# A convolution's later half moved into the gather stage, with the tiles of the recurrence reordered

## The reference, cut to what matters

```python
proj = h @ w_in[l]                       # hq, hf, hi, hg, cb, cc, ch, gates
...
o = hgrn2_chunkwise(rs(q), rs(k), rs(log_f), rs(hi))     # gated linear recurrence, chunks of 64
y_a = o_normed * silu(hg)
y_b = cb * causal_depthwise_conv(cc * ch, conv_w[l])     # 3 taps over positions, 512 channels
g_a, g_b = jnp.split(jax.nn.sigmoid(gates), 2, axis=-1)
merged = g_a * (y_a @ w_branch_hg[l]) + g_b * (y_b @ w_branch_conv[l])
x = x + merged @ w_out[l]
x = x + peer_ffn(rmsnorm_2(x, norm_ffn_g[l]), ...)

def peer_ffn(h, w_query, keys1, keys2, expert_u, expert_v):   # 8 heads, 2 x 128 keys, top 16
    q = (hf @ w_query).reshape(t, 8, 2, 128)
    s1, s2 = q[:, :, 0] . keys1, q[:, :, 1] . keys2
    v1, i1 = top_k(s1, 16); v2, i2 = top_k(s2, 16)            # then the best 16 of the 256 sums
    act = gelu(sum(expert_u[idx] * h))                        # 16384 experts, one row each of u and v
    out = sum(gate * act * expert_v[idx])
```

## Time and profile before

| what | us |
|---|---|
| median of 3 runs | 3173.85 (3169.38 to 3179.24) |
| profiled execution, its own time | 3174.83 |
| profiled execution, span of the trace | 3173.0 |
| start of level 1 of the mixer, from the span's start | 1516.35 |
| first gather issued, from the span's start | 1802.73 |

### The profile page before, as it was taken

One profiled execution on the slowest core, in us unless ns is written; L12 is line 12 of the kernel. 1 busy time (PEld: TensorE's weight loads), 2 busy tenths in 40 slices (PEclk: granted clock), 3 DMA queues, 4 the chain that ended last, 5 costly groups with the idle time before them and its releaser, 6 DMA issues. The chain is left out here.

```text
span 3173.0 us, 27344 instructions
## 1 busy us (share of the span) xinstructions
PE 2729.6 (86%) x9860; PEld 1403.3 (44%) x9860; DVE 1350.5 (43%) x3242; ACT 584.0 (18%) x1350; POOL 718.6 (23%) x622
## 2 busy tenths in 40 slices
PE   8999697787778878669999889999999877778887
PEld 6755333333333333244558756655555433333332
DVE  2162300000000000055422466676766777777774
ACT  2132100000000000012101123222322322222222
POOL 0000010000000000001440133443434444444442
PEclk9899799999999899879999999999999999999889
DMA  4003699999999999531114599999999999999997
GB/s 144 27 20 124 261 427 426 427 426 426 426 425 422 421 415 421 214 129 42 60 47 146 193 426 426 426 426 424 408 426 424 406 427 427 427 427 427 427 427 302
DMA packets 136982, 1043.17 MB, mean 329 GB/s; under 512 B 21824, under 2 KB 22672, under 8 KB 46352
## 3 DMA queue, kind: packets, MB, share of 16 engines
q0 software_dynamic: 82944, 545.32, 41.1%
q1 hardware_dynamic: 53904, 496.11, 38.2%
HBM read 1045.54 MB, written 20.97 MB: 336 GB/s over the span
## 5 line engine op out<-in xcount | busy, mean ns | idle before, releaser
L2132 PE MATMUL psum<-peer_ring,peer_diag 128*128 128x512 f32 x1824 | 861.2, 626 | 139.9 <-ACT peer_diag L2186 139.8
L2001 POOL DMA_INDIRECT peer_ring<-in_peer_uv,peer_pick x456 | 508.0, 1114 | 846.7 <-PE psum L2132 650.3
L2292 DVE CUSTOM_DVE_ANT_0 peer_ring<-peer_ring,sb_rows 128x1024 f32<-128x1024 f32 x456 | 556.9, 1225 | 327.7 <-DMA peer_ring<-in_peer_uv,peer_pick 319.8
L2132 PEld LDWEIGHTS psum<-peer_ring,peer_diag 128*128 128x128 f32 x1824 | 358.5, 200 | 603.1 <-issue 400.4
L1118 PE MATMUL psum<-ffn1w_w,sb_y 128*64 128x512 f32 x1872 | 509.6, 654 | 93.6 <-DMA ffn1w_w<-in_w_up 52.1
L1163 DVE TENSOR_TENSOR sb_y<-psum,sb_y 128x512 f32<-128x512 f32 x32 | 22.1, 692 | 877.0 <-ACT sb_y L1146 877.0
L1118 PEld LDWEIGHTS psum<-ffn1w_w,sb_y 128*64 128x64 f32 x1872 | 176.6, 149 | 361.0 <-issue 359.3
L2186 ACT ACTIVATE peer_diag<-sb_ident,peer_mix 128x128 f32<-128x128 f32 x512 | 177.4, 393 | 665.2 <-DVE peer_mix L2302 662.1
L1139 PE MATMUL psum<-ffn1w_w,moe_hT 128*64 128x512 f32 x864 | 227.9, 598 | 35.9 <-DVE moe_hT L1168 35.9
L1497 PE MATMUL psum<-sb_y,sb_tiles 128*128 128x512 f32 (+1 forms) x640 | 227.5, 514 | 19.2 <-PEq L104 18.5
L1211 POOL DMA_INDIRECT expert_rows<-sb_tiles,ffn_block_tok x32 | 32.2, 1007 | 894.8 <-ACT sb_tiles L1152 894.8
(11 more groups left out here) (427 smaller groups left out, 2697.6 us busy)
## 6 DMA issues: line engine op xcount, KB each, us to landing
ffn1w_w<-in_w_gate SPq DMA_DIRECT2D x64, 2048.0 KB, 33.1
ffn1w_w<-in_w_down SPq DMA_DIRECT2D x54, 2048.0 KB, 35.8
ffn1w_w<-in_w_up SPq DMA_DIRECT2D x53, 2048.0 KB, 33.9
sb_rows<-in_w_up SPq DMA_DIRECT2D x11, 2048.0 KB, 36.6
sb_tiles<-in_w_in2b SPq DMA_DIRECT2D x44, 512.0 KB, 3.4
sb_rows<-in_w_down SPq DMA_DIRECT2D x10, 2048.0 KB, 32.4
sb_tiles<-in_w_query SPq DMA_DIRECT2D x32, 512.0 KB, 7.7
sb_tiles<-in_w_out SPq DMA_DIRECT2D x24, 512.0 KB, 3.4
```

The costliest lines, as they stand in the source:

```text
L2001: pool.indirect_dma_start(out=row(n, 0, 2 * D), out_offset=None, in_=A["peer_uv"], in_offset=bass.IndirectOffsetOnAxis(ap=pick[:, i, j:j + ...
L2132: last = nc.tensor.matmul(ps[:, BANK[i] + c], diag[:, b % DIAGS, x], row(n, D + 512 * c, D + 512 * (c + 1)), start=False, stop=end, skip_g ...
L2292: dve.tensor_tensor_reduce(row(n, 0, D), row(n, 0, D), hr[:, i], 1.0, 0.0, ALU.mult, ALU.add, dots[:, i, j + x:j + x + 1]).then_inc(dotted, 1)
```

## The change

1. The convolution of the second half of the positions leaves the mixer. The 12 convolution tiles are multiplied at half width there; POOL works on 256 positions and keeps the last two columns of `cc * ch` in `halo`. In the gather stage the same 12 weight tiles are loaded again and multiplied with the second half's activations (`conv_product`); ACT copies `cc`, and DVE does the taps (`convolved`, six instructions per channel group).
2. In the mixer the first eight gate tiles now stand between the levels, ahead of the convolution tiles: one level has three half-width products rather than two of full width. Two convolution tiles are left for behind `outputs`, and eight gate tiles for behind the sums.
3. The first query's two tiles and its keys are loaded in the mixer, into the buffer that the attention scores leave, and are multiplied between the `result` tiles with the activations ahead of the norm (`first_query`); the norm's factor is applied to the query (`first_q`) and, at the start of the gather stage, to the activations in one DVE instruction of 128x2048.
4. In the gather stage 44 late jobs (12 convolution, 32 as before) stand at batches 4, 5, 7, 9, ... 79, four every seven batches; `late_sum` at 82; the second half's queries at 92, 96, 108, 112 and so on to 208, rather than 80 to 117. The ring of slots stays at ten throughout.
5. The results are written from other buffers, and their DMAs (0 and 1) stand in SP's program between query loads.

```diff
-    return keep + conv + gates + [A["w_br"][m] for m in range(KD)] + [A["w_out2"][m] for m in range(KD)]
+    return keep + gates[0:KD] + conv + gates[KD:] + [A["w_br"][m] for m in range(KD)] + [A["w_out2"][m] for m in range(KD)]
...
+                    if n == BR:
+                        sp.wait_ge(o_ps, KH)
+                        for side in range(2):
+                            sp.dma_start(query_w[:, side], A["w_query"][side]).then_inc(query_in, 16)
+                        sp.dma_start(first_keys, A["keys"][:, 0:2]).then_inc(query_in, 16)
...
+                def first_query(m):
+                    if m == 0:
+                        pe.wait_ge(query_in, 48)
+                    pe.wait_ge(raw, m + 1)
+                    for side in range(2):
+                        last = nc.tensor.matmul(ps[:, side, 0:HT], query_w[:, side, m], xn[:, m, 0:HT], start=m == 0, stop=m == KD - 1)
...
-                for n in range(NL):
+                for n in range(1, NL):
                     level(n, range(0, 2))
-                    product(CONV + 2 * n - 2)
+                    product(GA + 3 * n - 3)
+                    product(GA + 3 * n - 2)
                     level(n, range(2, NT))
-                    product(CONV + 2 * n - 1)
+                    product(GA + 3 * n - 1)
                 outputs()
-                product(GA)
-                product(GA + 1)
+                for n in range(GA + 3 * NL - 3, GB):
+                    product(n)
                 for p in range(KH):
                     sums(p)
-                for n in range(GA + 2, BR):
+                for n in range(GB, BR):
                     product(n)
...
+                for x in range(3 * NL - 3 - KD, 3 * KH):
+                    conv_copy(x)
                 for p in range(KH):
                     act.wait_ge(inv_ready, p + 1)
                     act.activation(K[:, 0, p], F[:, 0, p], ACT.Sqrt).then_inc(rs_ready, 1)
-                for m in range(4, KD):
-                    gate_copy(m)
                 act.activation(g, g, ACT.Silu).then_inc(silu_g, 1)
...
-    for j in range(LATE):
-        JOBS_AT.setdefault(6 + 2 * j, []).append(("late", j))
-    JOBS_AT.setdefault(71, []).append(("late_sum", 0))
+    for j in range(3 * KH + LATE):
+        JOBS_AT.setdefault(4 + 7 * j // 4, []).append(("conv", j) if j < 3 * KH else ("late", j - 3 * KH))
+    JOBS_AT.setdefault(82, []).append(("late_sum", 0))
...
-            slots = RING if n < 2 * BATCH * 80 else RING + 2 if n < 2 * PICKS else RING + 4
...
+                    if n >= RING:
+                        pool.wait_ge(spent, n - RING + 1)
+                    pool.indirect_dma_start(out=ring[:, slot], out_offset=None, in_=A["peer_uv"],
...
+                def convolved(p):
+                    n, w = place_of["conv", 3 * p + 2], core.vec[:, VEC["conv"]]
+                    dve.wait_ge(conv_copied, p + 1)
+                    dve.wait_ge(w_used[n % U], turns + n // U + 1)
+                    dve.tensor_copy(cc[:, 0:2], halo[:, p])
+                    step(dve.tensor_tensor(cc[:, 2:], conv_c[:], ps[:, 7, 0:HT], ALU.mult))
+                    step(dve.tensor_scalar(yb1[:, p], cc[:, 2:], w[:, 2 * KH + p:2 * KH + p + 1], None, ALU.mult))
+                    for back in (1, 2):
+                        ...
+                    dve.tensor_tensor(yb1[:, p], yb1[:, p], ps[:, 7, HT:], ALU.mult).then_inc(conv_done, 1)
```

More of the change, by code:

```diff
@@ L1630, in _ @@
                         next_sum(m - 2)
-                next_sum(KD - 2)
-                next_sum(KD - 1)
+                        first_query(m - 2)
+                for m in (KD - 2, KD - 1):
+                    next_sum(m)
+                    first_query(m)
             @block.scalar
@@ L1677, in _ @@
                         exponentials(n + 1)
-                    conv_copy(2 * n - 2)
-                    conv_copy(2 * n - 1)
-                act.wait_ge(conv_done, KH - 2)
+                    for x in range(3 * n - 3, 3 * n):
+                        if x < KD:
+                            gate_copy(x)
+                        else:
+                            conv_copy(x - KD)
                 for p in range(KH):
@@ L1957, in peer @@
             "lroot", "hn"))
-        landed = [st.sem(f"row{n}") for n in range(RING + 4)]
+        landed = [st.sem(f"row{n}") for n in range(RING)]
         w_ready, w_used, turns = core.w.ready, core.w.summed, core.w.turns
@@ L2031, in scores @@
                         for i in range(2):
-                            last = nc.tensor.matmul(ps[:, 5, (2 * s + i) * P:(2 * s + i + 1) * P], q[:, s, i * P:(i + 1) * P],
-                                                    keys[:, 2 * (r % H) + s], start=True, stop=True)
+                            qs, ks = (q[:, s], keys[:, 2 * (r % H) + s]) if r else (first_q[:, s], first_keys[:, s])
+                            last = nc.tensor.matmul(ps[:, 5, (2 * s + i) * P:(2 * s + i + 1) * P], qs[:, i * P:(i + 1) * P],
+                                                    ks, start=True, stop=True)
                     last.then_inc(s_ps, 1)
@@ L2055, in residual, with conv_product @@
                                          start=k % 4 == 0, stop=False, skip_group_check=True)
+                def conv_product(x):
+                    u, (p, part) = arrive("conv", x), (x // 3, x % 3)
+                    if part == 0 and p >= 1:
+                        pe.wait_ge(conv_copied, p)
+                    if part == 1 and p >= 1:
+                        pe.wait_ge(conv_done, p)
+                    o = ps[:, 6, 0:HT] if part == 0 else ps[:, 7, (part - 1) * HT:part * HT]
+                    for c in range(KD):
+                        last = nc.tensor.matmul(o, core.w.tiles[:, u, c], xn[:, c],
+                                                start=c == 0, stop=c == KD - 1)
+                    last.then_inc(w_used[u], 1)
                 def gate_product(m):
                     u = arrive("late", m)
+                    if m == 0:
+                        pe.wait_ge(conv_done, KH)
                     if m >= 2:
@@ L2092, in late_sum @@
                     last.then_inc(late_ss, 1)
-                query(0)
-                query(1)
+                scores(0)
+                pe.wait_ge(scaled, 1)
                 rows(0, 0)
-                scores(0)
                 rows(1, 2)
@@ L2361, in _ @@
                     for name, m in JOBS_AT.get(b - 2, ()):
-                        if name == "late" and BR <= m < OUT:
+                        if name == "conv" and m % 3 == 2:
+                            convolved(m // 3)
+                        elif name == "late" and BR <= m < OUT:
                             merge(m - BR)
```

160 lines of the change are left out of this document (89 added, 71 removed).

## The result

The changed kernel takes 3180.2 us (median of 20 runs, 3174.6 to 3184.7), the kernel before 3174.5 in 20 runs beside it. The ratio is 1.0017, its 95% interval 1.0011 to 1.0022: slower by a little, and within the 0.3% that were called "same". The forecast was 3163. The measured time lies inside the wide range of the prediction (3149 to 3183), but the kernel became slower where it was to become 11 us faster.

A forecast was written before the change was run, and what follows sets the result against it. It took TensorE to bound the mixer and DMA bytes the gather stage, with TensorE also full early there. 3173.0 - 33.8 + 14.8 + 7 + 1.5 = 3162.5 span, 3163 us as median; 8-in-10 range 3149 to 3183.

The forecast's parts named there:

- Levels: Mixer levels 1 to 6: less TensorE work takes them from 109.0 to 88.6 us, saving 20.4.
- behind the sums: Mixer, up to the first branch: fewer gate tiles, but TensorE idles 8.8 us and its clock drops; saves 9.5 us.
- first query: From mixer to first gather: query work moved earlier adds 6.0 us and saves 9.9, net 3.9 saved.
- Rival C: Mixer levels keep their pace, set by ACT, POOL and DVE: up to 20.4 us not saved, 3183 us; chance 0.14.
- Bytes: Gather stage: twelve 512 KB tiles loaded a second time, 6.29 MB at 425 GB/s, +14.8 us.
- Ring of ten: Gather stage: ten slots suffice for landing at 427 GB/s, but stalls have less cushion; +1.5 us, bounds -3 and +15.
- the base of the sum: Whole kernel: the profiled span of the kernel before, 3173.0 us, to which all savings and costs were applied.
- B: Batches 80 to 255: ten slots are too few and the DMA queue runs dry; slower, 3188 us; chance 0.17.
- TensorE in batches 4 to 79: Gather stage: TensorE needs 441.8 us against the DMA's 434, 8 short; +7 us, bounds 0 and 12.
- rival A: Gather stage: only the bytes count, the cushion hides TensorE's 8 us and stalls cost nothing: 3154 us; chance 0.22.
- landing time: Gathers after batch 128, from issue to landing: near 13 us at 427 GB/s.

The follow-up runs named there:

- e1: Changed kernel with `halo` taking 256 bytes per partition instead of 32, so the ring starts at a multiple of 256: 3156.2 us, ratio 0.9947 to the kernel before.
- e2: Kernel before with one unused tile of 32 bytes per partition put ahead of the ring: 3196.1 us, ratio 1.0075.
- g0: Changed kernel with ring, weight tiles and experts' ring on multiples of 256 bytes, plus ACT's new order of f4: 3140.9 us, ratio 0.9894 to the kernel before.
- f4: e1 with ACT's order behind the sums changed, two copies between the square roots, the sigmoid later: 3143.6 us, ratio 0.9904 to the kernel before.
- h3: g0 with convolution and late tiles every 1.5 batches instead of 1.75, ending at batch 68, not 79: 3151.4 us, ratio 0.9928 to the kernel before.
- e4: Kernel before with its ring kept at ten slots throughout: 3177.2 us, ratio 1.0012.

## Why the prediction was wrong

*Levels, behind the sums, first query:* right. The levels saved 20.6 us (20.4 forecast), the stretch from the outputs to the first branch 9.3 (9.5), that from there to the first gather 4.2 (3.9); level 0, now split by two products, gave 0.9 back, which had no term. In all 33.3 of 33.8. Rival C falls: the levels followed TensorE, though its 3183 came nearest to the measured time.

*Bytes:* the amount was right (6.3 MB, 14.7 us at 427 GB/s). **The step that failed is the rate of the gather stage:** "at 425 GB/s", "at 427 GB/s" in "Bytes in the gather stage" and "Ring of ten", and above all the base of the sum, 3173.0, in which the 569 MB that were there before keep their old time. The twelve new tiles alone would cost only 0.3 us more at the lower rate; it is the old rows that became slower, and the sum put that at nothing without a reason. The rates were carried over from the kernel before to a ring that starts elsewhere. The diff showed a new tile of eight numbers per partition ahead of the ring; I costed what it holds and not where it puts its neighbour. The runs showed 418 and 417 GB/s in its place (e1 and e2 move only addresses). In numbers: after lost 44.6 us against the bytes, e1 22.9, so the address is worth 21.7 us of span (22.8 with the 1.0 us by which e1's first gather came earlier), and 24.0 between the medians. No rival of the prediction had it either: B named the right sign and nearly the right size (3188) for another reason.

*TensorE in batches 4 to 79:* +7 forecast. Without the address (e1) the loss in batches 0 to 128 is 12.2 us against 10.8 before: +1.4, and in g0 none. Finer stretches of the same traces show that two things cancel. In batches 4 to 104, with the wait for `late_sum` at 82, before lost 5.2 us, e1 10.3, f4 and g0 8.4: +3 to +5, half of the forecast. In batches 104 to 128, from which the queries have moved away, before lost 4.1, e1 0.5, g0 1.2: -3 to -4, for which the sum had no term. The mechanism was right (h3), its size was half, and the total came near rival A by this second effect.

*Ring of ten:* +1.5 forecast. Of e1 against before it is (6.0 + 4.7) - (0.5 + 9.8) = +0.4, of e4 +2.6: in order, but in part by luck. The prediction reads the dip behind the first result's finish as one with twelve slots and the second finish as one with fourteen; both had ten, and so have both kernels there. What ten slots cost, 7.1 us from batch 160 on, and what they give back at the end, 4.7, had no terms. (Rival B's 268 MB are those of 128 batches; its place, batches 80 to 255, has 369, 16.5 us at its rates rather than 12.) The landing time, expected near 13 us, was 15.8 after, 14.7 in e1 and 14.4 with ten slots in the kernel before (2560 to 2665 us).

So the span of e1 comes out as 3173.0 - 34.3 + 14.7 + 1.4 + 0.4 = 3155.2, the measured one, and that of after as 3173.0 - 33.3 + 14.7 + 11.6 + 11.9 = 3177.9 (3178.0 measured). These sums say where the time went; that they close is no proof, since the loss is what is left of the time. On its boundary the change is worth 17.5 us; the 32 bytes took that and 6 us more.

## What to carry to other kernels

Before a small tile is put ahead of a large buffer that DMA writes, work out the byte at which the buffer starts: a multiple of 256 kept its rate, 32, 64 and 128 off it cost 1.3 to 1.7% of a stage bound by transfers. When the rate falls while the DMA share stays full, look at the lengths of the packets: if the median has grown (309 to 313 ns), look at addresses; if the median stands and a few per cent are very long (h3), look at rings, waits and engines. And where an engine's program puts long table work ahead of short copies that another engine waits for, move the copies: here this brought 12.6 us.

## What the runs showed of the hardware that I had not expected

- The address at which a row lands sets the length of its packet: 309 ns for 8 KB at a multiple of 256, a median of 313 and up to 324 at 32 bytes past it. Engines that read the same ring at the shifted address were not slower: PE's records of a batch's products have a median of 592 ns in before, after, e1 and e2, DVE's dot products a mean of 1225 or 1226.
- The price is not proportional: with half of the slots shifted it was 4 to 6 us, with all of them 22.
- Loads of 16 KB rows from SyncE's queue pay less: 613 against 611 ns in the median, 0.6% in the mean, and the rate rose from 426 to 429 GB/s. The median of 4 KB rows stayed at 159 ns.
- A DMA share of 1.00 does not say that no transfer is held up: at 408 GB/s (h3) and at 427 GB/s (before) it read 1.00 and 1.01.
- Fewer slots in the ring shorten the last stretch: the last six batches lost 9.8 us with fourteen slots and 5.1 with ten (e4). Why is open.
